# One chunk in two of the mixers' first products in three float32r products, its low half made by an adding transfer

## The reference, cut to what matters

```
h = rmsnorm(x, norm_mix[l])
(u_ssm, q_lat, kv_lat, k_rope, hg_q, hg_f, hg_i, hg_g, gate_logits) = split(h @ w_in[l])
```

## Time and profile before

| | us |
|---|---|
| median of 3 runs | 1895.93 |
| lowest, highest | 1893.66, 1900.63 |
| the profiled execution | 1899.83 |
| its span in the profile | 1898.0 |
| granted TensorE clock, mean of the span | 0.982 |

### The profile page before, as it was taken

One profiled execution on the slowest core, in us unless ns is written; L12 is line 12 of the kernel. 1 busy time (PEld: TensorE's weight loads), 2 busy tenths in 40 slices (PEclk: granted clock), 3 DMA queues, 4 the chain that ended last, 5 costly groups with the idle time before them and its releaser, 6 DMA issues.

```text
span 1898.0 us, 27088 instructions
## 1 busy us (share of the span) xinstructions
PE 1798.9 (95%) x10038; PEld 1445.6 (76%) x10038; DVE 1233.6 (65%) x1899; ACT 872.4 (46%) x1417; POOL 264.2 (14%) x266
## 2 busy tenths in 40 slices
PE   7999999989999999999989999998899999989998
PEld 6676676769998866667578998556799864779987
DVE  7996755545666992857455566665677646566775
ACT  4224445454444412345455445335555533555553
POOL 4015542020000003454012000100000000010000
PEclk9999999999999999999999999998999999799999
DMA  6444452445565444444245666431555544135554
GB/s 162 131 129 155 134 174 71 166 117 172 163 189 167 134 126 134 144 142 153 84 142 157 184 189 191 142 101 56 156 178 164 181 145 121 56 115 174 169 184 137
DMA packets 192359, 274.61 MB, mean 145 GB/s; under 512 B 25616, under 2 KB 129540, under 8 KB 192228
## 3 DMA queue, kind: packets, MB, share of 16 engines
q1 hardware_dynamic: 191364, 269.86, 46.3%
q0 software_dynamic: 864, 3.02, 0.5%
HBM read 271.78 MB, written 1.05 MB: 144 GB/s over the span
## 4 chain that ended last, share of the span: by engine, by line
PE 81%; DVE 8%; ACT 5%; issue 2%; SPq 1%; POOL 1%; DMA 0%; DVEq 0%; ACTq 0%; POOLq 0%
PE bank L401 47%; PE bank L399 24%; DVE WL L1175 2%; ACT WH L1462 2%; PE bank L674 2%; PE bank L588 1%; PE bank L596 1%; PE bank L1031 1%; PE bank L875 1%; PE bank L1051 1%; PE bank L490 1%; ACT HTH L1462 1%; DVE bank L2136 1%; DVE HTL L2083 1%; POOL WL L1175 1%
## 5 line engine op out<-in xcount | busy, mean ns | idle before, releaser
L1175 DVE TENSOR_TENSOR WL<-W,WH 128x1024 fp32r<-128x1024 f32 x308 | 377.5, 1226 | 254.0 <-ACT WH L1462 245.2
L1462 ACT ACTIVATE WH<-W 128x1024 fp32r<-128x1024 f32 x332 | 352.3, 1061 | 288.7 <-PE bank L401 255.6
L401 PE MATMUL bank<-HTH,WH 128*128 128x256 f32 x1536 | 439.0, 286 | 19.0 <-DVE WL L1175 8.9
L401 PE MATMUL bank<-HTL,WH 128*128 128x256 f32 x1536 | 435.1, 283 | 0.0
L401 PE MATMUL bank<-HTH,WL 128*128 128x256 f32 x1536 | 435.0, 283 | 0.0
L401 PEld LDWEIGHTS bank<-HTH,WH 128*128 128x128 f32 x1536 | 295.1, 192 | 24.7 <-DVE WL L1175 11.1
L401 PEld LDWEIGHTS bank<-HTL,WH 128*128 128x128 f32 x1536 | 295.3, 192 | 0.2
L401 PEld LDWEIGHTS bank<-HTH,WL 128*128 128x128 f32 x1536 | 295.1, 192 | 0.0
L401 PE MATMUL bank<-WH,HTL 128*128 128x512 f32 x672 | 262.0, 407 | 0.0
L401 PE MATMUL bank<-WH,HTH 128*128 128x512 f32 x480 | 194.7, 406 | 21.1 <-POOL WL L1175 5.7
L401 PE MATMUL bank<-WL,HTH 128*128 128x512 f32 x480 | 189.1, 394 | 0.0
(11 more groups left out here) (405 smaller groups left out, 2481.2 us busy)
## 6 DMA issues: line engine op xcount, KB each, us to landing
W<-in_w_in SPq DMA_DIRECT2D x132, 512.0 KB, 3.7
W<-in_ffn_w_gate_up SPq DMA_DIRECT2D x176, 256.0 KB, 3.4
W<-in_w_up SPq DMA_DIRECT2D x176, 256.0 KB, 3.6
W<-in_ffn_w_down SPq DMA_DIRECT2D x44, 512.0 KB, 4.3
W<-in_w_down SPq DMA_DIRECT2D x44, 512.0 KB, 3.5
W<-in_w_out SPq DMA_DIRECT2D x32, 512.0 KB, 3.4
W<-in_ssm_w_glu SPq DMA_DIRECT2D x16, 512.0 KB, 4.3
W<-in_x_w_kv SPq DMA_DIRECT2D x16, 512.0 KB, 3.7
```

The source lines that it names most:

```text
L401: m = pe.matmul(out, at_a(a[x]), at_b(b[y]), start=(start and i == 0), stop=(stop and i == 2), skip_group_check=True)
L1175: eng.tensor_tensor(WL[:, m % HSLOTS, 0:width], W[:, n % RSLOTS, 0:width], h, ALU.subtract)\
L1462: copy = lambda dst, src, scale=1.0: act.activation(dst, src, ACT.Copy, scale=scale)
```

## The change

In each pair of chunks of `hf`, `hq`, `hi`, `hg`, `kv` and `ql` the second one (`k0` of 2 and 6, for `hf` only 2) becomes an "added" chunk. It is loaded ahead of the first one of its pair and multiplied after it. ACT writes its negative, rounded to float32r, into `WL`, then copies the value into `WH`, and the raw slot is then free. POOL starts a transfer that reads the same chunk from HBM again and adds it onto `WL`, which leaves `W - WH` there. PE multiplies it in three float32r products with `mix_half`. For that, POOL makes `mix_half` at the start of the layer, right after `HTF` is scaled and the `u` products have ended; in layer 0 the memsets and `rope_angles` move behind the last of these transfers. ACT makes the first split of a layer right after its sine tables, and some evictions no longer call `split_to`.

```diff
         def low_done(m):
-            who = "dve" if splits[m][1] == "dve" else "pool"
-            return f"low_{who}", sum(1 for _, w in splits[:m + 1] if (w == "dve") == (who == "dve"))
+            who = splits[m][1]
+            if who == "dma":
+                return f"low_dma{m % HSLOTS}", 16 * sum(1 for _, w in splits[m % HSLOTS:m + 1:HSLOTS] if w == "dma")
...
+            def declare(name, srcs, k, cols, low="dve"):
                 n = len(chunks)
                 chunks.append((name, srcs, k, cols))
+                if low is not None:
+                    m = split_of[n] = len(splits)
+                    splits.append((n, low))
+                    chunk_release[n] = ("high", high_done(m)) if low == "dma" else low_done(m)
+                return n
+            def operands(n):
...
+                m = split_of[n]
+                if splits[m][1] == "dma":
+                    pe.wait_ge(sem["high"], high_done(m))
                 s, v = low_done(m)
                 pe.wait_ge(sem[s], v)
+                return [shaped(w, m % HSLOTS) for w in (WH, WL)]
+            def in_pairs(tag, wname, l, K, c0, cols, kstep, added):
+                n = {}
+                for k0 in range(0, K, 2 * kstep):
+                    for k in (k0 + kstep, k0):
+                        n[k] = declare(tag, rows(wname, l, k, kstep, c0, cols), kstep, cols, "dma" if k in added else None)
+                    yield n[k0]
+                    yield n[k0 + kstep]
...
+                    if added:
+                        n = next(numbers)
+                        if k0 in added:
+                            src, slot = halves, half_slot
+                            pe.wait_ge(sem["mix_halves"], l + 1)
+                        w = operands(n)
...
+                                         halves=mix_half, added=(2,) if name == "hf" else (2, 6))
...
-                pe.wait_ge(sem["mix_halves"], l + 1)
                 for n in range(2):
...
+            def add_chunk(m):
+                n, _ = splits[m]
+                _, (src,), k, cols = chunks[n]
+                pool.wait_ge(sem["negative"], negative_done(m))
+                dst = WL[:, m % HSLOTS, 0:k * cols].rearrange("p (k n) -> p k n", k=k)
+                pool.dma_start(dst, src, accum_op=ALU.add).then_inc(sem[low_done(m)[0]], 16)
...
                     later_consts()
+                pool.wait_ge(sem["mix_scaled"], l + 1)
+                wait_full(pool, ("u", l, 3))
+                signal(halves_of(mix_half, HTF, 2, 6), "mix_halves", l + 1)
+                split_to(split_before["ql", l, 1])
+                if l == 0:
                     for j in range(ROPE // 2):
...
-                signal(halves_of(mix_half, HTF, 2, 6), "mix_halves", l + 1)
                 split_to(split_before["gate", l, 5, 1])
...
+                    if who == "dma":
+                        signal(copy(WL[:, m % HSLOTS, 0:width], W[:, n % RSLOTS, 0:width], -1.0), "negative", negative_done(m))
                     signal(copy(WH[:, m % HSLOTS, 0:width], W[:, n % RSLOTS, 0:width]), "high", high_done(m))
...
+            def first_added(l):
+                split_to(split_before["u", l, 3] + 1)
...
-                    full("bu", l, q, j)
+                    wait_full(act, ("bu", l, q, j), split_to if q >= 2 else None)
...
                 for q in range(2):
                     tables(l, q)
+                if l == 0:
+                    first_added(l)
                 if l:
-                    evict(RB, "rb", mix_norm, width=S)
+                    evict(RB, "rb", mix_norm, width=S, split=False)
                     tables(l, 2)
+                    first_added(l)
                     take_bu(l, 0)
```

More of the change, by code:

```diff
@@ L407, in token_out, with token_steps @@
                     pass
-            def token_steps(tag, wname, l, act, K, c0, cols, low="dve", kstep=2, halves=None):
+            def token_steps(tag, wname, l, act, K, c0, cols, low="dve", kstep=2, halves=None, added=()):
                 ps = [begin(*tag, tt) for tt in range(TT)]
+                if added:
+                    numbers = in_pairs(tag, wname, l, K, c0, cols, kstep, added)
                 for k0 in range(0, K, kstep):
                     src, slot = act, lambda k: k
-                    if halves and k0 // kstep % 2:
+                    if added:
+                        n = next(numbers)
+                        if k0 in added:
+                            src, slot = halves, half_slot
+                        w = operands(n)
+                    elif halves and k0 // kstep % 2:
                         n, w = chunk(tag, rows(wname, l, k0, kstep, c0, cols), kstep, cols, "both")
@@ L523, in feature_out, with feature_steps @@
                     pass
-            def feature_steps(tag, wname, l, act, K, c0, tiles, low="dve", kstep=2, extra=0):
+            def feature_steps(tag, wname, l, act, K, c0, tiles, low="dve", kstep=2, extra=0, halves=None, added=()):
                 cols = tiles * P + extra
@@ L530, in feature_steps @@
                     kr = begin(*tag, "kr")
+                if added:
+                    numbers = in_pairs(tag, wname, l, K, c0, cols, kstep, added)
                 for k0 in range(0, K, kstep):
-                    n, w = chunk(tag, rows(wname, l, k0, kstep, c0, cols), kstep, cols,
-                                 low[k0 // kstep] if isinstance(low, tuple) else low)
+                    src, slot = act, lambda k: k
+                    if added:
+                        n = next(numbers)
+                        if k0 in added:
+                            src, slot = halves, half_slot
+                            pe.wait_ge(sem["mix_halves"], l + 1)
+                        w = operands(n)
+                    else:
+                        n, w = chunk(tag, rows(wname, l, k0, kstep, c0, cols), kstep, cols,
+                                     low[k0 // kstep] if isinstance(low, tuple) else low)
                     need_rows(act, k0 + kstep)
@@ L705, in mixer_in @@
                 def mixer_in(name, c0, tiles, extra=0):
-                    return feature_steps((name, l), "w_in", l, HTF, KT, c0, tiles, low=None, extra=extra)
+                    return feature_steps((name, l), "w_in", l, HTF, KT, c0, tiles, low=None, extra=extra,
+                                         halves=mix_half, added=(2,) if name == "hf" else (2, 6))
                 def mixer_tokens(name, c0):
-                    token_out((name, l), "w_in", l, HTF, KT, c0, 512, low=None)
+                    token_out((name, l), "w_in", l, HTF, KT, c0, 512, low=None, halves=mix_half, added=(2, 6))
                 def ssm_u(*qs):
@@ L1665, in ssm_weights @@
                 for c in range(2):
-                    evict(BT[:, :, c, :], "bT", l, c)
+                    evict(BT[:, :, c, :], "bT", l, c, split=False)
             def take_bu(l, q):
@@ L1747, in _ @@
                     ssm_weights(0)
-                    evict(PAR[:, C2:C3], "par2", width=DEPTH * NR2)
+                    evict(PAR[:, C2:C3], "par2", width=DEPTH * NR2, split=False)
                     take_bu(l, 0)
```

33 lines of the change are left out of this document (20 added, 13 removed).

## The result

| | before | after |
|---|---|---|
| median of the runs made side by side (4 each) | 1898.28 | 1939.22 |
| lowest, highest after | | 1936.29, 1940.26 |
| the profiled execution | 1899.83 | 1940.09 |
| its span | 1898.0 | 1938.3 |
| mean granted clock | 0.982 | 0.969 |

The change makes the kernel slower by 2.1%: the ratio is 1.0214, with a 95% interval of 1.0185 to 1.0243. The forecast was 1900.6 with a range up to 1912. It was wrong, and not by a little: 41 us came where 5 were expected.

The account below looks back on a forecast made before the run. PE, busy for 95% of the span, was taken as the bound. Waits of 7.7, 4.4 and 2.8 us plus 1.0 for the clock, less 11.2 saved, gave +4.7 on the 1895.9 median: 1900.6 us, range 1889 to 1912.

Parts of the forecast that it names:

- Saving: On PE, converted chunks as three float32r products: 5.6 us per layer, 11.2 us off in both, ends 10.2 and 12.4.
- Term 2: Front of layer 0: ACT's first split delays the evictions of `bT`, and `hf` behind them, by 4.4 us; ends 2.1 and 5.5.
- Term 1: Front of layer 1: PE waits 7.7 us for `hf`'s added chunk, issued after POOL's halves; ends 5.2 and 10.7.
- T: Time of an adding transfer from POOL's issue to landing: 6.2 us taken, ends 3.7 and 9.2.
- near -2: What the forecast's sum would be, in place of about +5 us, with the skill's 4.4 us for an adding transfer.
- Term 3: `hq`'s second added chunk, raw slot freed only when `hf` ends: PE waits 1.4 us per layer, 2.8 in all.
- Term 4: Lower PE clock after a stop of 7.7 us: 1 us lost, ends 0 and 3.4.
- Costed at nothing: Later added chunks, ACT's extra copies, POOL's moved angles and halves, and added DMA traffic: all taken as covered, 0 us.
- the 5 us of cover: Layer 0: POOL's moved memsets and angles, 23 us long, end near 127, ahead of `lssq` near 133.
- (a): Rival: the adding transfer is slow, lengthening PE's waits in `hf` and `hq`; 1910.6 us at T = 9.2; chance 0.33.
- point of decision: T = 7.8 us, from which the slow-transfer rival decides because the forecast's sum passes +9.5 us.
- Rival (c): DVE starves POOL while it writes transfer descriptors, so issue and T are long; slower, near 1912 us; chance 0.03.

## Why the prediction was wrong

**Saving.** 11.2 us forecast. Where it can be read by itself it is right: 2.76 for `hi` and `hg` (2.8), 1.0 for `ql` in layer 0 (1.2), 0.24 lost per `kv` chunk (0.1 taken, 0.35 as the bound).

**Term 2, the front of layer 0, is the step that failed.** It was costed as 4.4 us, by ACT's first split "between the tables and the evictions of `bT`". ACT's first split was not there, and the front of this document has its place wrong too. It was at `parameters()`, which stands earlier in the same program and calls `split_to` through `full`. The stop was 18.64 us and PE's delay 18.4. The rows that would have shown it were all there: the load of that chunk is issued at 28.04 and the parameters are taken at 14.84. I had listed the calls of `split_to` that the diff touches, and not those which it leaves alone but which now find something to split. With that call gone the step as costed took 2.4 in place of 4.4.

**Term 1**: 7.7 forecast, 9.58 measured; within its ends. The halves took 6.6 in place of 5.0, beside a busy DVE. In layer 0, where no wait was forecast, one of 1.16 came: `hf` began 1.8 us after the halves were done (54.09), not 5.8. POOL's program order was indeed the cause: the run that issues the add first cut the stop to 2.9.

**T**: 6.2 forecast, 7.4 measured at the median, 4.8 to 8.9. The plain copy took 4.8 (my 5.2 from the two rows was near), and the addition 2.6 where I had 1.0 for the second read. The Trainium skill's account (DMA: Bandwidth & Descriptors, "Anatomy of one DMA", with Collectives: The Full Stack, "The bandwidth ceiling") gave an estimate of 4.4, with an addition that costs no cycles of its own. The 4.8 and the 7.4 are both longer, and the 2.6 between the two runs are more than a second read alone was put at. Both were taken beside loads, and no run shows whether the rest is the addition itself or the full engines. The prediction's "near -2" for the sum with 4.4 is a slip: term 1 would be 5.9 and term 3 nothing, and the sum +0.1.

**Term 3**: 1.4 forecast, 2.9 and 3.3 measured, as T was longer and the load before it too (a median of 5.2 us to landing around 50 to 80 us in the run with one added chunk in `hq`, against 3.7).

**Term 4, the clock, was too small.** 1 us was taken, 3.4 the upper end. Three of the stops in `hf` and `hq` were each followed by 1.7 to 2.5 us lost at a lower clock (5.2, 5.4 and 4.5 for 2.88), 6.5 together. The cross-attention of layer 1, unchanged, took 6 us longer with a lower clock in it; the three profiles with a stop of 7.5 to 9.6 us in layer 1 all have 50.8 or 50.9 us there, and eight of the ten other kernels run 44.8. How the one would reach the other is not shown.

**Costed at nothing.** ACT's extra copies were costed by their busy time and by DVE's slack. What they do is stand in front of evictions. In the changed kernel itself this shows once, at `par`; in the kernels with fewer added chunks it was the largest term, 11 to 14 us. POOL's angles took 33 us beside DVE, not 23, so the 5 us of cover were gone (they ended at 158.9, and `lssq` was there at 155.2), but the run which puts them back shows no gain. POOL's halves beside DVE were costed at nothing too; in the run with POOL's part alone they made `CT` late by 2 us. And DVE's wait after the fourth scan of layer 1 was to shrink by some 8 us; it went from 19.86 to 18.39. The upper end of the saving, 12.4, does not follow from its own bound (11.7 and four times 0.5 are 13.7); nothing hangs on it.

**The rivals.** The side of (a) was right, slower than the bound, but not its reason: with T at 7.4 it was below its own point of decision, and taking the addition away wins 7 us of 41, in one execution. Rival (c) had its sign in the trace of before, which the earlier trace rows leaves out: the second of the four operations, at 137.03, took 2.13 us beside DVE, and the last one 1.27. But the issue instructions stayed short (1.2 us each, 1.7 at most). No rival had ACT waiting for a load ahead of the parameters.

**The 41 us, as the runs give them** (from ratio to ratio, in us of the kernel before): the split at `par` 17; the order of POOL's first add, with its clock, 15; `hf`'s added chunk as such 3; `hq`'s second added chunk, once the eviction stands ahead of the split, 4; together 40. The first two are clear of the noise. The 3 and the 4 are not: the intervals on both sides of each step overlap. With those gone the change is worth nothing: 1.0004, with some 8 us of saving left in its products. What takes these back is in part seen (the move on POOL, 4 us by itself, with its 2.4 for `CT`; 3.2 for transfers) and in part open. No version here is shown to beat the kernel before.

## What to carry to other kernels

When an edit puts a new kind of work into a shared list, go through every place that draws from the list, the untouched ones first, and ask of each whether the work is ready there; an in-order engine that stops for a load it will need later holds up all that it already could do. Where work is taken ahead of an eviction, take it only if its input has surely landed, and otherwise empty the bank first. And when the bound engine stops, count the stop and the slow stretch that may follow it.

## What was not expected of the hardware

An adding transfer took 7.4 us from issue to landing at the median (18 of 512 KB and four of 288 KB), against 4.8 for the plain one in the same place. Beside loads it filled the DMA engines: their share was 1.02 to 1.11 at 238 to 277 GB/s. That is 216 to 270 GB/s for a full share, where the plain loads of before moved 151 at 0.54, or 280. POOL's subtraction of 128 by 512 values took 2.13 us beside DVE's large two-input operations and 1.27 to 1.32 otherwise. DVE's operations beside it were longer as well: 2.18 us for 1.23, and 1.14 for 0.19. And a bank that is freed late shows in PE's waits as "issue": what holds it is found in the timeline of the engine that empties it.
